# First pair's page attention run between the dense tiles of layer one's projections, with keys and values loaded apart

## What is computed

```
proj = h @ w_in                       # 1024 -> 2048: u (512) | q | k | v of 4 heads, 2 x 64 wide
a_out = pool_mix(u, pool_hist, ...)   # running means over 2, 4, 8, 16 tokens, then a small matrix per group
# differential attention; samples attend to 2048 past tokens in 16 pages each, found by page_table
k_past = kv_past[:, :, 0]; v_past = kv_past[:, :, 1]
logits = concat(q . k_past, q . k) * HD_B ** -0.5
p = softmax(logits); a = p[:, :, 0] - lam * p[:, :, 1]
o_b = rmsnorm(a @ v, subln_g) * (1.0 - lam_init)
y = concat([a_out, o_b]) @ w_out
```

## Time and profile before

| | |
|---|---|
| median of three runs | 1770.05 us (1755.3 to 1776.97) |
| the profiled execution | 1765.39 us, its span 1763.8 us |
| projections of layer one, tiles 4 to 15 | about 50 to 128 us of the span |
| page attention | about 134 to 332 us |
| TensorE busy, whole span | 96% |

### The profile page before, as it was taken

How to read it: one execution, slowest core, us unless ns; L and a number is a source line. 1 busy time by engine, 2 the same in 40 slices (tenths; PEclk the granted TensorE clock), 3 DMA queues, 4 the chain that set the end, 5 groups by cost and what they waited for, 6 DMA issues and landing times.

```text
span 1763.8 us, 37514 instructions
## 1 busy us (share of the span) xinstructions
PE 1698.0 (96%) x14699; PEld 1582.9 (90%) x14699; DVE 1150.3 (65%) x1902; ACT 727.1 (41%) x1525; POOL 154.5 (9%) x212
## 2 busy tenths in 40 slices
PE   7997999899999999999999999999999999989998
PEld 6995666799999999999899898878799999989998
DVE  4335776687567766664588874677678766566655
ACT  4114555545344544441521413453234554345443
POOL 0710000220000000020000000012002000000002
PEclk9999999999999999999999999999999999999999
DMA  8219999436766676634368677622133677522222
GB/s 281 73 38 350 354 350 345 157 115 238 260 257 234 252 280 248 227 127 143 99 192 297 214 253 269 203 96 85 49 127 120 229 270 260 201 72 77 95 72 78
DMA packets 150791, 339.00 MB, mean 192 GB/s; under 512 B 9178, under 2 KB 83732, under 8 KB 149053
## 3 DMA queue, kind: packets, MB, share of 16 engines
q1 hardware_dynamic: 148307, 249.74, 41.5%
q0 software_dynamic: 2240, 87.41, 12.6%
q10 hardware_dynamic: 114, 0.03, 0.0%
HBM read 324.36 MB, written 100.19 MB: 241 GB/s over the span
## 4 chain that ended last, share of the span: by engine, by line
PE 83%; DVE 7%; DMA 4%; ACT 3%; issue 2%; SPq 1%; DVEq 0%; ACTq 0%
PE pp L826 21%; PE pp L1118 17%; PE pp L809 16%; PE pp L755 13%; DMA raw<-in_w_down 3%; PE pp L868 2%; PE pp L1067 1%; DMA kvring<-in_cache_b_kv 1%; PE pp L1225 1%; PE pp L882 1%; PE pp L902 1%; PE pp L1272 1%; PE pp L1250 1%; PE pp L1321 1%; DVE stat L1963 1%
## 5 line engine op out<-in xcount | busy, mean ns | idle before, releaser
L2239 ACT ACTIVATE whi<-raw 128x1024 fp32r<-128x1024 f32 x88 | 93.3, 1060 | 335.5 <-PE pp L1118 197.3
L1588 DVE TENSOR_TENSOR x<-x,pp 128x576 f32<-128x576 f32 x128 | 96.5, 754 | 150.6 <-PE pp L826 150.4
L1118 PE MATMUL pp<-a_hi,whi 128*128 128x288 f32 x768 | 177.7, 313 | 0.3 <-DVE proj L1902 0.3
L1118 PE MATMUL pp<-a_hi,wlo 128*128 128x288 f32 x768 | 164.5, 296 | 0.0
L1118 PE MATMUL pp<-a_lo,whi 128*128 128x288 f32 x768 | 164.0, 295 | 0.0
L1118 PEld LDWEIGHTS pp<-a_hi,whi 128*128 128x128 f32 x768 | 124.5, 190 | 26.6 <-issue 23.0
L809 PE MATMUL pp<-t_hi,u_lo 128*128 128x288 f32 x448 | 132.6, 296 | 0.0
L809 PE MATMUL pp<-t_lo,u_hi 128*128 128x288 f32 x448 | 132.5, 296 | 0.0
L809 PE MATMUL pp<-t_hi,u_hi 128*128 128x288 f32 x448 | 132.0, 295 | 0.0
L1118 PEld LDWEIGHTS pp<-a_lo,whi 128*128 128x128 f32 x768 | 123.6, 189 | 0.0
L1118 PEld LDWEIGHTS pp<-a_hi,wlo 128*128 128x128 f32 x768 | 123.5, 189 | 0.0
(11 more groups left out here) (376 smaller groups left out, 4267.8 us busy)
## 6 DMA issues: line engine op xcount, KB each, us to landing
kvring<-in_cache_b_kv SPq DMA_DIRECT2D x128, 512.0 KB, 6.0
out_new_d_sample<-in_cache_d_kv POOLq DMA_DIRECT2D x32, 2040.0 KB, 8.4
raw<-in_w_up SPq DMA_DIRECT2D x32, 1024.0 KB, 5.5
raw<-in_w_down SPq DMA_DIRECT2D x32, 1024.0 KB, 7.1
kring<-in_cache_d_kv SPq DMA_DIRECT2D x104, 256.0 KB, 3.5
vring<-in_cache_d_kv SPq DMA_DIRECT2D x104, 256.0 KB, 5.3
raw<-in_w_in_cd SPq DMA_DIRECT2D x24, 1024.0 KB, 5.3
out_new_d_sample<-in_cache_d_kv POOLq DMA_DIRECT2D x8, 2016.0 KB, 9.1
```

What stands on the lines that cost most here:

```text
L1118: last = pe.matmul(acc_h[s][:, h, :], w[s][:, k, :], m[:, k, NH * h:NH * h + NH], start=(k == 0 and n == 0), stop=(k == KT_N - 1 and n == 2))
L1588: dve.tensor_tensor(xt, xt, acc_h[n % 2], ALU.add).then_inc(acc_free, 1)
L2239: act.activation(whi_v[j], raw_v[q // 2][:, :, j, :], ACT.Copy).then_inc(whi_ready, 1)
```

## The change

The first eight steps of the page attention (pair 0, all its blocks of pages) run within the projections: TensorE does tile T = 4 + i in step i, where the prompt's work stood. The other 28 steps stay behind token_major. For this, tiles 0 to 3 are now the queries and 4 to 7 u; the queries are scaled after the first group and staged by GpSimd at once, for pairs 0 and 1. The pooling on GpSimd waits until tiles 8 to 11 (the keys) are out and for the rows of u, which TensorE now transposes behind tile 12. In the early steps keys and values come by DMAs of their own, 256 KB a page, into two buffers each (on b_hi and b_lo), and other banks and buffers are used: scores in bank 7, weights in the second half of bank 6, keys through banks 4 and 5. The prompt's stages start at step 8 and stand 5 s // 4 apart. The core of the diff (lines that only name other buffers or pass `steps` left out):

```diff
+        early_k, early_v = ([at(f"early_{n}{i}", W_B + o + 2048 * i, 2048)[:, :].rearrange("p (g f) -> p g f", g=4)
+                             for i in range(2)] for n, o in (("k", 0), ("v", 4096)))
+        kt_early = [at("kt_early0", W_V, 2048)[:, :].rearrange("p (i g n) -> p i g n", i=4, g=4),
+                    at("kt_early1", W_PROJ + 12 * N, 2048)[:, :].rearrange("p (i g n) -> p i g n", i=4, g=4)]
...
+        EARLY = NB0 - 1
+        AB_TILES = (4, 5, 6, 7, 0, 1, 2, 3) + tuple(range(8, 16))
+        EARLY_STEPS = [(0, i) for i in range(EARLY)]
+        LATER_STEPS = [(0, EARLY)] + [(j, i) for j in range(1, NP) for i in range(NB0)]
+        early = lambda j, i: j == 0 and i < EARLY
+        SCORES, OUTPUT = (bank[2], bank[7]), bank[6][:, 0:2 * P]
+        WEIGHTS = (bank[3], bank[6][:, 2 * P:4 * P])
+        keys_bank = lambda j, i, p: bank[(4 if early(j, i) else 0) + p % 2]
+        keys_buffer = lambda j, i: (kt_early if early(j, i) else kt_sa)[i % 2]
...
             for s in range(last + 1):
-                if m == first + 7 * s // 4:
+                if m == first + 7 + 5 * s // 4:
                     stage(s)
...
+        def load_early(eng, i, v):
+
+            if i >= 2 and v:
+                eng.wait_ge(S0["o_ps"], i - 1)
+            elif i >= 2:
+                eng.wait_ge(S0["kt_ps"], 4 * (i - 1))
+            for p in range(4):
+                page = page_of(eng, 0, i, p)
+                eng.dma_start((early_v if v else early_k)[i % 2][:, p, :],
+                              a["cache_b_kv"][0][ds(page, 1), :, v, :, :].rearrange("o t h e -> (o t) (h e)")
+                              ).then_inc(S0[f"kv{2 * v + i % 2}{p // 2}"], 16)
...
-            if i >= 4 or not isinstance(j, int) or j:
+            if isinstance(j, int) and j == 1 and i < 4:
+                eng.wait_ge(*((S0["kt_ps"], 4 * EARLY), (S0["o_ps"], EARLY), (tile_done, T_AB + 16), (tile_done, T_AB + 16))[i])
+            else:
                 eng.wait_ge(S0["o_ps"], j * NB0 + (i - 3 if i >= 4 else i - 4))
...
-            return (2 * j + i // 4 + 1) * 32
+            return (2 * j + 2 + i // 4 + 1) * 32
...
+                for i in range(4, EARLY):
+                    load_block(sp, 1, i)
+                with sp.Fori(2, NP) as j:
+                    for i in range(EARLY):
                         load_block(sp, j, i)
 
-                each_pair(sp, pair)
+            def ab_unit(n):
+
+                unit(w_ab, (512, 768, 0, 256, 1024, 1280, 1536, 1792)[n], n, n % 2, wait=(n >= 2))
...
-            load_block(sp, 0, 0)
-            load_block(sp, 0, 1)
-            matrix(w_ab, T_AB, 16, first=1)
+            for i in range(2):
+                load_early(sp, i, 0)
+                load_early(sp, i, 1)
+            ab_unit(2)
+            ab_unit(3)
+            load_early(sp, 2, 0)
+            ab_unit(4)
+            load_early(sp, 3, 0)
+            for i in range(2, EARLY):
+                load_early(sp, i, 1)
+                if i + 2 < EARLY:
+                    load_early(sp, i + 2, 0)
+                if i in (3, 5, 7):
+                    ab_unit(5 + (i - 3) // 2)
+            load_block(sp, 1, 0)
+            load_block(sp, 1, 1)
             sp.wait_ge(rows_done, 1)
             sp.dma_start(a["new_pool_prompt"][0, 0], e2[0][49:64, :]).then_inc(rows_out, 16)
             sp.dma_start(a["new_pool_sample"][0][:, 7:15, :], e2[0][NS:P, :]).then_inc(rows_out, 16)
...
+            load_block(sp, 1, 2)
+            load_block(sp, 1, 3)
             store_tokens(0, a["new_bkv_prompt"], a["new_bkv_sample"], 0)
-            sp.wait_ge(tile_done, T_AB + 16)
             cache_blocks()
...
-                            pe.wait_ge(S[f"kv{i % 4}{p // 2}"], loaded(j, i))
+                            if early(j, i):
+                                pe.wait_ge(S[f"kv{i % 2}{p // 2}"], (i // 2 + 1) * 32)
+                            else:
+                                pe.wait_ge(S[f"kv{i % 4}{p // 2}"], loaded(j, i))
                         at_least(pe, S[("kt_a", "kt_d")[p % 2]], j * 16 + (2 * i + p // 2))
...
+                    elif j == 0:
+                        pe.wait_ge(qs_saved, 2)
...
                     pe.wait_ge(S["e"], j * NB0 + (i + 1))
+                    if early(j, i) and i:
+                        pe.wait_ge(S["o"], i)
...
+                if steps == EARLY_STEPS:
+                    keys(0, 0, (0, 1, 2, 3))
+                for j, i in steps:
+                    scores(j, i)
+                    keys_beside(j, i, keys, (0, 1))
+                    if i and (j, i) != LATER_STEPS[0]:
+                        values(j, i - 1)
+                    elif j:
+                        values(j - 1, NB0 - 1)
+                    keys_beside(j, i, keys, (2, 3))
+                    other_work(NB0 * j + i)
+                    weights(j, i)
+                if steps == EARLY_STEPS:
+                    ab_tile(T_AB + 12)
+                values(*steps[-1])
...
+            def ab_tile(T):
+
+                pe.wait_ge(wlo_ready, T + 1)
+                pe.wait_ge(acc_free, T + 1)
+                for k in range(KT_N):
+                    for n, (w, m) in enumerate(((whi_v, ahk), (whi_v, alk), (wlo_v, ahk))):
+                        for h in range(2):
+                            last = pe.matmul(acc_h[T % 2][:, h, :], w[T % 2][:, k, :], m[:, k, NH * h:NH * h + NH],
+                                             start=(k == 0 and n == 0), stop=(k == KT_N - 1 and n == 2))
+                last.then_inc(tile_done, 1)
+
+            pe.wait_ge(hist_done, 1)
+            sample_attention(EARLY_STEPS, lambda m: ab_tile(T_AB + 4 + m))
             for i in range(4):
                 last = pe.transpose(bank[7][:, P * i:P * i + P], pk[:, i, N - P:N], ident)
             last.then_inc(rows_ps, 1)
-            dense(lambda i: i + 1, 3, ahk, alk, a_ready, 0)
+            for T in range(T_AB + 13, T_AB + 16):
+                ab_tile(T)
             pe.wait_ge(acc_free, 2 + T_AB + 16)
-            pe.wait_ge(hist_done, 1)
+            pe.wait_ge(S0["o"], EARLY)
...
+            dve.wait_ge(acc_free, 2 + T_AB + 4)
+            dve.tensor_scalar(proj[:, 4 * N:8 * N], proj[:, 4 * N:8 * N], 0.125, None, ALU.mult).then_inc(gains_q, 1)
+
+            def ab_result(T):
+
+                if T_AB + 6 <= T + 1 < T_AB + 16:
+                    split_lo((T + 1) // 4, (T + 1) % 4)
+                dve.wait_ge(tile_done, T + 1)
+                dst = pk[:, AB_TILES[T - T_AB], :].rearrange("p (h c) -> p h c", h=2)
+                dve.tensor_tensor(dst, acc_h[T % 2], r_h, ALU.mult).then_inc(acc_free, 1)
+
+            sample_attention(EARLY_STEPS, orun0, samp0, lambda m: ab_result(T_AB + 4 + m))
             dve.wait_ge(rows_ps, 1)
             dve.tensor_copy(e2[0][:, :], bank[7]).then_inc(rows_done, 1)
-            dense(lambda i: i + 1, 2, to_proj(1))
-            dense(lambda i: i + 3, 1, to_proj(3), last=True)
-            dve.wait_ge(acc_free, 2 + T_AB + 16)
-            dve.tensor_scalar(proj[:, 4 * N:8 * N], proj[:, 4 * N:8 * N], 0.125, None, ALU.mult).then_inc(gains_q, 1)
+            for T in range(T_AB + 13, T_AB + 16):
+                ab_result(T)
             token_major(0, 0)
...
+                    if steps == EARLY_STEPS:
+                        other_work(i)
+                    act.wait_ge(S["pt_ps"], j * NB0 + (i + 1))
+                    n, rows = len(chunks(i)), P if i < NB0 - 1 else NS
+                    act.activation(pt_l0[i % 2][0:rows, 0:P * n], WEIGHTS[early(j, i)][0:rows, 0:P * n],
+                                   ACT.Copy).then_inc(S["pt"], 1)
+                    if steps != EARLY_STEPS:
                         other_work(NB0 * j + i)
 
...
+            def ab_weights(T):
+
+                if T_AB + 6 <= T < T_AB + 16:
+                    act.wait_ge(tile_done, T - 1)
+                    split_hi(T // 4, T % 4)
+
+            sample_attention(EARLY_STEPS, samp0, lambda m: ab_weights(T_AB + 5 + m))
+            for T in range(T_AB + 13, T_AB + 16):
+                ab_weights(T)
...
+            pool.wait_ge(gains_q, 2)
+            pool.tensor_copy(q_s[:, 0, :, :], pk[:, 4:8, SEQ:N]).then_inc(qs_saved, 1)
+            pool.wait_ge(qs_saved, 1)
+            stage_queries((0, 1))
             pool.wait_ge(hist_done, 1)
+            pool.wait_ge(acc_free, 2 + T_AB + 12)
+            pool.tensor_copy(k_s[:, 0, :, :], pk[:, 8:12, SEQ:N]).then_inc(qs_saved, 1)
             pool.wait_ge(rows_ps, 1)
...
                 pool.tensor_tensor(u, m[:, 16:528], u, ALU.subtract).then_inc(pm_ready, 1)
-            pool.wait_ge(gains_q, 2)
-            save_samples(0, 4, 8)
             pool.wait_ge(pm_ready, 4)
-            stage_queries()
+            stage_queries((2, 3))
```

More of the change, by code:

```diff
@@ L590, in cache_blocks @@
             def cache_blocks():
-                def pair(j):
-                    for i in range(2 if isinstance(j, int) and j == 0 else 0, NB0 - 1):
+                for i in range(4, EARLY):
```

(77 more changed lines are left out.)

64 lines of the change are left out of this document (25 added, 39 removed).

## The result

The median of five runs is 1786.34 us (1774.38 to 1790.3). The ratio to the kernel before is 1.0085, with a 95% interval of 1.0048 to 1.0121: a little slower, within 2%. The forecast was 1775.6 us. The profiled execution took 1774.38 us and was the fastest of the five; its span is 1772.8, 9.0 us more than before, where the prediction had 5.6.

The account below looks back on a forecast made before the run. TensorE was taken as nearly full in both projections and page attention. The steps sum to +5.6 us at the output projection, so the profiled 1765.4 becomes 1771.0, plus 4.7 for the median: 1775.6 us; forecast 1766 to 1785, range 1757 to 1795.

Parts of the forecast that it names:

- The sum: All steps up to the output projection's first tile: it starts at 337.6 us instead of 332.0, +5.6 us.
- The opening: After group one, TensorE waits for history copy, key transposes and staged queries; first scores at about 57.7 us.
- Eight steps with a tile each: Early page steps beside dense tiles: 86.2 us including 0.4 us of pauses a step; last dense tile ends at 171.1.
- the stalls go: Rival: early steps without pauses and half of the attention's later waits gone, 1766.6 us, down to 1757; chance 0.25.
- What was costed at nothing: In the early steps: page loads, the tiles' weights and GpSimd's later pooling are covered and add no time.
- The join: After the last dense tile, k_tok stores queue behind eight page loads; pair 1's scores start at 188.0, without the wait 181.6.
- Twenty-seven steps: Tenth step to output projection: prompt stages packed into 19 steps add 5.5 us, 144.1 becomes 149.6; bounds 141.5 to 157.6.
- VectorE as a bound: Rival: VectorE's work and waits exceed TensorE's in 18 dense steps, +13 to +18 us, 1788 to 1794; chance 0.14.
- The ring: Rival: the ring of four blocks loses its lead; 24 blocks each 1.5 us late, +36 us, 1812; chance 0.04.
- late keys: Rival: keys come late in the early steps and each tile waits, 3 us a step, 1800 us; chance 0.03.
- The ceiling: TensorE's idle time in the page attention, 204.0 - 183.0 = 21 us or 1.2%, is the most that can be gained.

Follow-up runs that it names:

- experiment 1: Changed kernel with the token stores issued ahead of the loads of blocks 2 and 3 of pair 1; median 1780.09 us, ratio 1.0079.
- experiment 7: Changed kernel with only the two k_tok stores ahead of pair 1's blocks 2 and 3, and the lambda arithmetic moved earlier; one time, 1774.82 us.
- Experiment 3: Kernel before with one line changed: the prompt's stages start at step 8 and stand 5 s // 4 apart; median 1778.28 us, ratio 1.0048.
- experiment 5: Changed kernel with the prompt's product and VectorE's copy of it moved ahead of key pages 2 and 3 in the step; one time, 1780.41 us.
- experiment 6: Changed kernel with ScalarE's prompt work done in the next step behind the copy of key page 0, up to step 26; one time, 1786.97 us.
- the best kernel: Changed kernel with k_tok stores first, earlier lambda arithmetic, product ahead of key pages 2 and 3, and one prompt stage per step; median 1757.1 us, ratio 0.9945.
- experiment 9: Kernel before with only the prompt's product and VectorE's copy of it moved ahead of key pages 2 and 3; median 1770.72 us, ratio 1.001.
- experiment 8: Changed kernel with k_tok stores first, earlier lambda arithmetic, and the product ahead of key pages 2 and 3; median 1764.56 us, ratio 0.9968.

## Why the prediction was right, and where its sum was off

The forecast held in its main argument. TensorE is the bound in both stretches, and moved loads don't pay by themselves: DMA lost a hundredth of the chain and TensorE took it. The sum was 5.6 us; the mark says 11.9, and the medians say 16.3 (the interval of the ratio is 8.5 to 21.4 us, so the sum lies below it). The 4.4 us between mark and medians lie behind the mark or in executions without a trace, and nothing here shows where. The time, 1786.34, lies in the range of 1757 to 1795, but outside the forecast's own 1766 to 1785, which had a chance of 0.52, and below VectorE's 1788. That the range held it is owed to its taking in that rival, and to some luck, for the rival's mechanism isn't what happened. By the steps of the sum:

*The opening* (predicted 57.7, was 59.49). The order of events is the predicted one. The history's copy came at 54.43 instead of 53.35, and the window 49.5 to 60 has a clock of 0.84: the 16 transposes take 3.49 us. The clock's fall was named as possible; neither is in the sum. Share of the miss: +1.8.

*Eight steps with a tile each.* No pauses at all: 10.66 us a step, which is 6.4 + 4.36 less 0.1, where 0.4 was allowed for pauses. The rival that the stalls go was right here, by 0.5 us a step. The last tile ends 1.7 us early in spite of the late opening, so these steps are worth -3.5. What was costed at nothing cost nothing: no wait for a page, a tile's weights or the pooling. The DMA share is 0.59 where 0.7 was expected.

*The join* (predicted 188.0, was 190.20). The wait on SyncE's queue was named with its place, its cause and who is queued behind it, and experiment 1 shows it: without the loads ahead, 10.55 us less. From the end of the last tile to the scores of m = 9 it is 20.8 us, where the sum had 16.9: the second store went out 1.1 us later than it had it, the landing was taken at 6.0 us and was 6.97, and from the end of the wait to the scores it took 3.0 us for 1.5, of which 1.1 are the clock. +3.9. The Trainium skill's "DMA: Bandwidth & Descriptors", section Queues, rings and completion order, says that a DMA engine consumes one ring's descriptors in order; the runs agree as far as they go. Stores behind the eight loads landed after 6.8 to 8.5 us (here and in experiment 7), those with no load ahead after 2.0 to 2.4 (experiment 1) or 2.1 to 4.5; shared bandwidth without any order would look alike. The Trainium skill's "TensorE: Matmul & The Clock Gate", Part 1, says that the clock falls to half when TensorE idles, and the trace agrees: 0.50 from 180.95 to 191.15, and from 54.70 to 58.05 at the end of the opening's pause and behind it.

*Twenty-seven steps* (predicted 149.6, were 153.74): this is the step that failed, and with +4.1 us the largest part of the miss. Its first half was near: TensorE's busy time grew by 6.9 us (133.81 to 140.73) for 5.5 in the sum, 0.5 of it the slow clock of m = 9. Its second half took the pauses for unchanged, and they grew from 10.3 to 13.0 us. 3.0 are the new wait for the product's copy; ScalarE's keys went from 4.0 to 5.8, VectorE's from 3.4 to 0.9. The prediction looked for VectorE as a bound by its busy time (112 of 154 us: it is none) and not for a bank that VectorE hands back within a step. Experiment 3 has 9.1 us of this in a kernel without the change, experiment 5 takes 4.4 of them away, and experiment 6 has 2.1 of these from ScalarE's order alone. The upper bound, 157.6, held it.

The rivals: *the stalls go* is true for the early steps, where it gives 4 us, and wrong for the later ones. *VectorE as a bound* named one of the two engines and the wrong mechanism: 3 us of an order within the step, not 13 to 18 of busy time. *The ring* and *late keys* are refuted: no matmul waits for a page in after from 60 to 345 us, though experiment 1 shows what a block that is asked for 10 us late costs (2.3 us in step m = 10). *The ceiling* of 21 us stands; the best kernel gets 7.4 of them.

Open: part of each mend comes back as another pause (in experiment 9 all of it), and which waits can go together wasn't settled. A bank of its own for the prompt's product wasn't tried on the chip.

## What to carry to other kernels

Before you move loads from a stage that looks bound by DMA under one that has DMA to spare, read TensorE's busy time in both: its idle time is all that can be won. Then ask what stood in the stage's pauses for nothing (here prompt work in the first nine steps) and where it goes now, since packed into full steps it costs its whole price, and can add a wait where a bank is wanted back within the step. And look at each issuing queue at the seam: here two stores that an engine waits for stood behind 4 MB of loads, worth 10.6 us with the slow clock behind the pause, and moving just those two ahead won it back. When two runs differ by a few us, compare the granted clock of the stretch and the single steps before you believe the sum: in experiment 6 a slow stretch of 3.35 us hid a gain of 2.1.

## What was not expected of the hardware

Within a pause of 9.9 us the clock fell to 1.2 GHz, and it stayed there for the first 4 us of work behind the pause, which cost 1.5 us on top; the 1.8 us before 148.36 had left no trace. The clock also fell where TensorE had just had several short pauses (0.89, 0.72 and 0.23 us ahead of 330.19 in experiment 6, the same three in experiment 1), while with the same three pauses it stayed at 2.4 GHz in the kernel after; what decides that isn't shown. A weight unit of 1 MB, which the page of after gives as 7.1 us from issue to landing, took 25.05 us in experiment 8, while the core's DMA share fell to 0.24 (1510 to 1515 us): on the mean of its engines DMA had time to spare, so the cause is open. Splitting the pages' loads into keys and values brought no wait for a page: from 60 to 170 us their landing took 3.1 to 3.3 us at the median for 256 KB, where the page gives 5.5 for 512 KB.
